# Norms and transposes of the heads moved from a stage of their own into the input projection

## What is computed

```
xn = rms_norm(x, norm_attn_g)
z  = einsum('btd,de->bte', xn, w_in)
(qa, ck, cv, sk, sv, wk, wv, ng, fq, fk, fv, ff, ga, gb) = split(z, offs, axis=-1)
qa = rms_norm(heads(qa, 8), q_norm_a_g)
sk = rms_norm(heads(sk, 2), k_norm_sel_g);  wk = rms_norm(heads(wk, 2), k_norm_win_g)
ng = sigmoid(ng)
fq = rms_norm(heads(fq, 8), q_norm_b_g);    fk = rms_norm(heads(fk, 8), k_norm_b_g)
logf = log_sigmoid(ff + b_forget)
```

## Time and profile before

| | |
|---|---|
| median of 3 runs | 964.01 us (961.81 to 964.22) |
| the profiled execution | 960.74 us, span 958.0 us |
| TensorE busy | 862.8 us, 90% of the span |
| VectorE busy | 529.6 us, 55% |
| ScalarE busy | 366.2 us, 38% |
| GpSimd busy | 158.3 us, 17% |
| mean granted TensorE clock | 0.969 |

### The profile page before, as it was taken

The page is one execution under the profiler, slowest core; times in us unless marked ns, Lnnn a source line. Parts: engine busy times, 40 slices in busy tenths (PEclk is TensorE's granted clock), DMA queues, the critical chain, the costliest instruction groups (busy, mean ns, idle before and its releaser), DMA issues. The chain is left out here.

```text
span 958.0 us, 18143 instructions
## 1 busy us (share of the span) xinstructions
PE 862.8 (90%) x7225; PEld 708.5 (74%) x7225; DVE 529.6 (55%) x982; ACT 366.2 (38%) x657; POOL 158.3 (17%) x261
## 2 busy tenths in 40 slices
PE   2899638879999999999999978899979999999996
PEld 1788427778988997665665546899569898899984
DVE  5544377863353386674456634564755665565654
ACT  2232365543242332453223441443334443444430
POOL 0000313301112112323344430000001111010100
PEclk9899878999999999999999999999979999999999
DMA  6342196116532447999999997878034644465411
GB/s 212 122 153 92 28 282 228 45 53 154 155 133 90 177 164 318 358 328 346 414 410 416 396 400 267 244 211 298 11 103 159 199 155 131 149 205 171 131 44 59
DMA packets 90590, 191.86 MB, mean 200 GB/s; under 512 B 7418, under 2 KB 68634, under 8 KB 78138
## 3 DMA queue, kind: packets, MB, share of 16 engines
q0 software_dynamic: 15408, 106.04, 28.9%
q1 hardware_dynamic: 73820, 84.43, 28.5%
q10 hardware_dynamic: 1296, 0.45, 0.2%
HBM read 187.44 MB, written 7.64 MB: 204 GB/s over the span
## 5 line engine op out<-in xcount | busy, mean ns | idle before, releaser
L1472 PEld LDWEIGHTS banks<-consts_base,stream_rows 128*128 128x128 f32 x672 | 73.2, 141 | 31.0 <-issue 28.2
L1719 ACT ACTIVATE keys_turned<-banks 128x512 f32<-128x512 f32 x94 | 54.8, 596 | 100.6 <-PE banks L1472 98.3
L258 PE MATMUL banks<-tokens_turned_high,w_gates_high 128*128 128x288 f32 x288 | 86.4, 300 | 3.5 <-PEq L191 2.3
L1472 PE MATMUL banks<-consts_base,stream_rows 128*128 128x128 f32 x672 | 82.5, 275 | 4.7 <-PEq L191 1.7
L259 PE MATMUL banks<-tokens_turned_low,w_gates_high 128*128 128x288 f32 x288 | 85.3, 296 | 0.0
L1011 PE MATMUL banks<-chunks_turned_high,cmp_w_high 64*128 64x256 f32 (+1 forms) x512 | 77.3, 296 | 5.3 <-DVE cmp_w_low L251 2.7
L260 PE MATMUL banks<-tokens_turned_high,w_gates_low 128*128 128x288 f32 x272 | 81.6, 300 | 0.0
L1011 PE MATMUL banks<-chunks_turned_low,cmp_w_high 64*128 64x256 f32 (+1 forms) x512 | 74.3, 284 | 0.0
L1011 PE MATMUL banks<-chunks_turned_high,cmp_w_low 64*128 64x256 f32 (+1 forms) x512 | 74.2, 283 | 0.0
L1700 DVE COPY keys_turned<-banks 128x512 f32<-128x512 f32 x74 | 50.3, 690 | 28.5 <-PE banks L1472 21.5
L251 DVE TENSOR_TENSOR chunks_turned_low<-banks,chunks_turned_high 128x512 fp32r<-128x512 f32 x64 | 41.1, 684 | 42.3 <-ACT chunks_turned_high L246 42.3
(11 more groups left out here) (445 smaller groups left out, 2110.6 us busy)
## 6 DMA issues: line engine op xcount, KB each, us to landing
w_up_gate<-in_w_up SPq DMA_DIRECT2D x12, 1024.0 KB, 7.3
w_up_gate<-in_w_gate SPq DMA_DIRECT2D x12, 1024.0 KB, 9.9
w_down<-in_w_down SPq DMA_DIRECT2D x12, 1024.0 KB, 5.1
w_in_slot<-in_w_in SPq DMA_DIRECT2D x8, 1424.0 KB, 6.2
w_gates<-in_w_in SPq DMA_DIRECT2D x10, 512.0 KB, 7.4
cmp_w<-in_cmp_w_k SPq DMA_DIRECT2D x4, 512.0 KB, 20.2
cmp_w<-in_cmp_w_v SPq DMA_DIRECT2D x4, 512.0 KB
stream_rows<-in_state_win_k SPq DMA_DIRECT2D x8, 256.0 KB
```

Of the source, the lines that this page charges most:

```text
L258: nc.tensor.matmul(out, lh, rh, start=start, stop=False, **kw)
L1472: ins = nc.tensor.transpose(bank(t)[:, q * P:(q + 1) * P], src, ident)
L1719: copy = lambda a, b: nc.scalar.activation(a, b, ACT.Copy)
```

## The change

`stage_heads` is gone. Chunks of the projection come in the order 3, 4, 5, 6, 0, 1, 2, 7, so that the forget-branch queries (FQ), its keys (FK), the other queries (QA) and the two other keys (KK) are complete after the third, fourth, sixth and seventh chunk. The loop of chunks is written out. Each chunk folds its own sample rows between its two prompt tiles. Squares, sums, roots, scalings and transposes of a group follow in the programs of the engines during the next chunks; KK is turned after the last chunk, and the turned forget-branch keys are evacuated by ScalarE. Row numbers are worked out after the second chunk.

In the token stage each row tile has a semaphore of its own, only the scaling waits for the gain, and ScalarE makes the high part of the first chunk as its last step. The loads of gains and the small loads of the compression network are issued during the first chunks, the masks of the prompt stage after the last chunk's load. GpSimd sets the sample rows to zero; its four gathers wait until the last chunk's queries are turned, since they write where the `w_in` slots now lie.

`load_w1` opens SyncE's program of the prompt stage. The forget gate's exponential and logarithm stand at the start of ScalarE's program there, its subtraction before the fourth unit on DVE, its running sums before the thirteenth unit on PE. The store of `logf` comes last, and GpSimd's copy of those columns waits for it, ahead of the gathers of old forget gates.

```diff
-def stage_tokens(c, w, w_loaded):
+def stage_tokens(c, z_at, w, w_loaded, wh, high):
...
-            sp.dma_start(x[:, 0:2, :], d["x_prompt"].rearrange("b (t p) d -> p (b t) d", p=P)).then_inc(tokens_in, 16)
-            sp.dma_start(x[0:NS, 2, :], d["x_sample"].rearrange("b s d -> (b s) d")).then_inc(tokens_in, 16)
-            sp.dma_start(gain[:, :], d["norm_attn_g"].to_broadcast([P, D])).then_inc(tokens_in, 16)
+            for t in range(2):
+                sp.dma_start(x[:, t, :], d["x_prompt"][0, t * P:(t + 1) * P, :]).then_inc(tokens_in[t], 16)
+            sp.dma_start(x[0:NS, 2, :], d["x_sample"].rearrange("b s d -> (b s) d")).then_inc(tokens_in[2], 16)
+            sp.dma_start(gain[:, :], d["norm_attn_g"].to_broadcast([P, D])).then_inc(gain_in, 16)
...
+                load_w_in(c, sp, w, w_loaded, u, ORDER[u] * ZC)
...
+            act.wait_ge(w_loaded[0], 16)
+            split_high(nc, wh[0][:, :, :], w[0][:, :, :]).then_inc(high, 1)
...
-            dve.wait_ge(tokens_in, 48)
...
+                dve.wait_ge(tokens_in[t], 16)
...
+            dve.wait_ge(gain_in, 16)
...
-            dve.wait_ge(pages_in, 16 * DB)
...
+ORDER = (3, 4, 5, 6, 0, 1, 2, 7)
...
+    groups = {"FQ": ((O_FQ, NH),), "FK": ((O_FK, NH),), "QA": ((O_QA, NH),), "KK": KK}
+    complete = {"FQ": 2, "FK": 3, "QA": 5, "KK": 6}
...
+                sp.wait_ge(z_sums, 3 * n - 5)
+                sp.wait_ge(low, n - 1)
+                load_w_in(c, sp, w, w_loaded, n % 2, at(n))
+                if n == 2:
+                    chunks.load_small(sp)
+            c.load_prompt(sp)
...
+            nc.gpsimd.memset(z[:, 2, :], 0.0).then_inc(zeroed, 1)
             nc.gpsimd.memset(c.qp[:, :, :], 0.0)
             nc.gpsimd.memset(c.fqp[:, :, :], 0.0)
...
+            pool.wait_ge(low, NZC)
+            pool.wait_ge(z_sums, 3 * NZC - 2)
+            pool.wait_ge(heads_turned, number["QA", 2])
             for m in range(NB):
                 chunks.gather(m)
...
+                    ins = nc.tensor.transpose(U[bank][:, r * P:(r + 1) * P], src, c.k("ident"))
+                ins.then_inc(heads_turned, 1)
...
+                u, tok = n % 2, slice(t * P, (t + 1) * P)
+                for k in range(KD):
+                    m = product(nc, U[3 * u + t][:, 0:ZC], (c.fTh[:, k, tok], c.fTl[:, k, tok]), (wh[u][:, k, :], wl[u][:, k, :]),
+                                start=(k == 0), stop=(k == KD - 1))
+                m.then_inc(z_sums, 1)
...
+            for n in range(NZC):
+                u = n % 2
+                if n >= 2:
+                    pe.wait_ge(z_out[0], 2 * n - 2)
+                    pe.wait_ge(z_out[1], n - 1)
+                    pe.wait_ge(fold_out, n - 1)
+                pe.wait_ge(w_loaded[u], n // 2 * 16 + 16)
+                for k in range(KD):
+                    g = k % 4
+                    m = nc.tensor.matmul(U[3 * u + 2][32 * g:32 * g + 32, 0:ZC], c.xsT[:, k, :], w[u][:, k, :], start=(k < 4), stop=(k >= 4))
+                m.then_inc(z_sums, 1)
+                pe.wait_ge(low, n + 1)
+                tokens(n, 0)
+                pe.wait_ge(z_out[0], 2 * n + 1)
+                nc.tensor.matmul(U[3 * u + 2][0:NS, 0:ZC], c.k("fold"), part[u], start=True, stop=True).then_inc(folded, 1)
+                if n == 5:
+                    turn(("FQ", 2))
+                if n == 6:
+                    turn(("FK", 1))
+                    turn(("FK", 2))
+                if n == 7:
+                    for t in range(3):
+                        turn(("QA", t))
+                    turn_tails()
+                tokens(n, 1)
+                if n == 1:
+                    move_row_numbers()
+                if n == 4:
+                    turn(("FQ", 0))
+                    turn(("FQ", 1))
+                if n == 5:
+                    turn(("FK", 0))
+            turn_nsa_keys()
...
+            def square(group):
...
+                act.wait_ge(fold_out, n + 1)
+                if rank[group]:
+                    act.wait_ge(sumsq, rank[group])
                 for t in range(3):
...
+                    for j, (off, heads) in enumerate(groups[group]):
+                        ins = nc.scalar.activation(sq[:, t, j * heads:(j + 1) * heads, :], by_head(t, off, heads), ACT.Square)
+                ins.then_inc(squares, 1)
+
+            def root(group):
+                act.wait_ge(sumsq, rank[group] + 1)
+                lo, n = rs_at[group], sum(heads for _, heads in groups[group])
+                nc.scalar.activation(rs[:, :, lo:lo + n], rs[:, :, lo:lo + n], ACT.Sqrt, scale=1.0 / HD, bias=c.eps[:, :]).then_inc(roots, 1)
...
+            for n in range(NZC):
+                if n == 5:
+                    queries("FQ", 0)
+                if n == 6:
+                    fox_keys(0)
+                if n + 1 < NZC:
+                    split(n + 1)
+                if n == 3:
+                    square("FQ")
+                    root("FQ")
+                if n == 4:
+                    square("FK")
+                    root("FK")
+                if n == 5:
+                    queries("FQ", 1)
+                    queries("FQ", 2)
+                if n == 6:
+                    square("QA")
+                    root("QA")
+                    fox_keys(1)
+                    fox_keys(2)
+                if n == 7:
+                    square("KK")
+                    root("KK")
+                    for t in range(3):
+                        queries("QA", t)
...
+                        nc.scalar.activation(chunks.tails[0:HD, m, :, 0:2], U[2][0:HD, m * 2 * CS:(m + 1) * 2 * CS].rearrange("p (x s) -> p s x", x=2), ACT.Copy)
+                    nc.scalar.activation(z[:, :, O_NG:O_NG + 3 * NH], z[:, :, O_NG:O_NG + 3 * NH], ACT.Sigmoid).then_inc(branch_gates, 1)
+                rows1(n)
...
+            def sample_part(n):
+                dve.wait_ge(z_sums, 3 * n + 1)
+                if n >= 2:
+                    dve.wait_ge(folded, n - 1)
+                nc.vector.tensor_copy(part[n % 2], U[3 * (n % 2) + 2][:, 0:ZC]).then_inc(z_out[0], 1)
+
+            def rows0(n):
+                dve.wait_ge(z_sums, 3 * n + 2)
+                nc.vector.tensor_copy(z[:, 0, cols_of(n)], U[3 * (n % 2)][:, 0:ZC]).then_inc(z_out[0], 1)
...
+            def sum_squares(group):
+                dve.wait_ge(squares, rank[group] + 1)
+                lo, n = rs_at[group], sum(heads for _, heads in groups[group])
+                nc.vector.tensor_reduce(rs[:, :, lo:lo + n], sq[:, :, 0:n, :], AX.X, ALU.add).then_inc(sumsq, 1)
...
+            split(0)
+            for n in range(NZC):
+                sample_part(n)
+                if n == 5:
+                    gain_keys("FK")
+                if n + 1 < NZC:
+                    split(n + 1)
+                if n == 1:
+                    row_numbers()
+                if n == 2:
+                    dve.wait_ge(rows_moved, 1)
+                    nc.vector.tensor_copy(c.quarter_row[:, :], U[7][:, 2 * P:2 * P + DB])
+                if n == 3:
+                    sum_squares("FQ")
+                if n == 4:
+                    sum_squares("FK")
+                if n == 6:
+                    sum_squares("QA")
+                if n == 7:
+                    sum_squares("KK")
+                rows0(n)
+                sample_rows(n)
+                if n == 3:
+                    scale("FQ")
+                if n == 4:
+                    scale("FK")
+                if n == 6:
+                    scale("QA")
+                if n == 7:
+                    scale("KK")
+                    gain_keys("KK")
+            forget_parts()
...
-            load_constants(sp)
+            chunks.load_w1(sp, 0)
...
-                                 ("fox_k", O_FK, FW), ("fox_v", O_FV, FW), ("logf", O_FF, NH), ("win_k", O_WK, KVW), ("win_v", O_WV, KVW)):
...
+                if name == "logf":
+                    sp.wait_ge(logf_ready, 1)
...
+                if off == O_FF:
+                    pool.wait_ge(logf_ready, 1)
...
+                if n == 12:
+                    pe.wait_ge(logf_ready, 2)
...
+                    nc.tensor.matmul(c.ps[6][:, NH:2 * NH], up[:, 0:P], lf[:, 1], start=False, stop=True).then_inc(cum_ready, 1)
...
+            nc.scalar.activation(c.forget_abs[:, :, :], c.forget_abs[:, :, :], ACT.Exp, scale=-1.0).then_inc(fl_ready, 1)
+            act.wait_ge(fl_ready, 1)
+            nc.scalar.activation(c.forget_abs[:, :, :], c.forget_abs[:, :, :], ACT.Ln, bias=1.0).then_inc(fl_ready, 1)
...
-            dve.wait_ge(masks_in, 16)
-            dve.wait_ge(cum_ready, 1)
-            link(nc.vector.tensor_copy(cq[:, :, :], c.ps[6][:, 0:2 * NH].rearrange("p (t h) -> p t h", t=2)))
+            dve.wait_ge(c.prompt_in, 16)
...
+                if n == 3:
+                    ff = z[:, :, O_FF:O_FF + NH]
+                    dve.wait_ge(fl_ready, 2)
```

(55 more changed lines are left out.)

386 lines of the change are left out of this document (167 added, 219 removed).

## The result

The changed kernel took **945.63 us** (median; 944.90 to 945.72, four runs) against 964.12 us for the kernel before (961.81 to 964.96, four runs): ratio 0.9824, 95% interval 0.9803 to 0.9845, 18.5 us less. The forecast was 939.3, 24.7 less. The profiled execution took 945.58 us, its span is 943.7, mean clock 0.976.

The account below looks back on a forecast made before the run. PE bounds the projection, while DVE and ScalarE take turns in the heads stage. Terms -23.3 up to the prompt stage's start, then -2.6 and +1.2, make -24.7: from 964.0 to 939.3 us, range for 8 in 10 933 to 946.5.

Parts of the forecast that it names:

- step 3: End of the projection: gathers end in time, prompt stage starts at 117.0 instead of 140.3 us; sum so far -23.3.
- queue rival: Projection chunks: group work waiting in DVE's and ScalarE's queues holds PE, some 8 us, giving 947; chance 0.12.
- Step 1: Token stage: DVE's first low part starts at once, first token matmul at 26.1 instead of 29.3 us; -3.2.
- Step 2: Projection chunks: folds, transposes and row numbers paid whole on PE; last token matmul ends at 113.5 us, +9.7.
- bounded this only on the side of a gain: First chunk, within the token step: up to 1.4 us more gain if PE's clock rises sooner.
- Step 4: Prompt stage: first exponential at +4.4 instead of +7.0 us, -2.6; added running sums and small operations, +1.2.
- rival by which table switches leave idle time: ScalarE's four exposed table loads: idle stretches of up to 1.4 us each, giving 944.8; chance 0.04.

Follow-up runs that it names:

- e1: The changed kernel with GpSimd's four gathers moved from the end of the projection to the prompt stage; 935.42 us, ratio 0.9727.
- e4: The kernel before with the token stage's part of the change alone, zeroing of `z` still on VectorE; 960.61 us, ratio 0.9991.
- e5: e4 with the zeroing of z's sample rows moved from VectorE to GpSimd at the projection's start; 960.52 us, ratio 0.9960.
- s14: The kernel of e1 run again, unedited, beside the changed kernel on one chip; 935.43 us, ratio 0.9719.
- e11: The kernel of e1 run again, unedited, in another set; 941.57 us, ratio 0.9763.
- e2: The changed kernel with only two of the four gathers moved to the prompt stage; 939.28 us, ratio 0.9769.
- e3: The kernel before with one added wait that holds its four gathers until near the heads stage's end; 976.58 us, ratio 1.0148.
- e8: e1 with four plain 1 MB loads added, issued by GpSimd at the projection's end; 947.65 us, ratio 0.9853.
- e9: e1 with four plain 1 MB loads added, issued by SyncE at the projection's end; 942.77 us, ratio 0.9787.
- s13: The changed kernel run again, unedited, beside the kernel of e1 on one chip; 945.31 us, ratio 0.9820.

## Why the prediction was off by 6 us

**Where it failed: step 3**, in the sentence "POOL's four gathers ... start once QA is turned and end before that", which put their cost at nothing. Their issue did end before (115.3), their landing did not. The prompt stage came at 125.25 instead of 117.0, 8.2 us late; e1 took the gathers out of this place and the stage started at 117.37. The step counted GpSimd as an engine with 4.0 us of work, where the barrier counts it until its transfers are in. The trace of the kernel before would have given it: its gathers took 9.4 us to land by the median and 14.3 at most, which from an issue at 114.35 gives 124 to 129. None of the rivals had this mechanism. The range (933 to 946.5) reached 945.6 because of the queue rival, which didn't come, so it is luck that the measured time lies inside it.

**Step 1 was right as a sum and incomplete as a reason.** First token matmul forecast at 26.1, measured 26.12; ScalarE's high part forecast at 19.0, measured 19.59. The text said that what is won is that the low part starts at once. It does so only because the zeroing of `z` has left VectorE (e4: -0.8 us without that, e5: -2.9 with it).

```profile
19.59 2.58 ACT L246 ACTIVATE w_in_high<-w_in_slot 128x2848 fp32r<-128x2848 f32 x1 [2.44 <-DMA w_in_slot<-in_w_in]
23.35 2.58 ACT L246 ACTIVATE w_in_high<-w_in_slot 128x2848 fp32r<-128x2848 f32 x1 [1.19 <-DMA w_in_slot<-in_w_in]
...
22.94 3.12 DVE L251 TENSOR_TENSOR w_in_low<-w_in_slot,w_in_high 128x2848 fp32r<-128x2848 f32 x1 [4.94 <-PEq L191]
...
26.12 0.66 PE L258 MATMUL banks<-w_in_high,tokens_turned_high 128*128 128x356 f32 x1 [0.58 <-DVE w_in_low L251]
```

**Step 2 was right from the second chunk on.** Last token matmul forecast to end at 113.5, measured 113.82 + 0.33 = 114.15. The first chunk ends at 37.09 where 38.59 - 3.2 + 0.75 = 36.14 was forecast, 0.95 late, of which the others give 0.3 back: its token matmuls follow each other every 0.295 us, the spacing of the lower clock level, from 26.12 to 30.73, for 4.6 us; in the kernel before that phase was 2.8 us long. The forecast had bounded this only on the side of a gain. The other chunks took 77.06 us where 77.35 was forecast. In them PE is busy throughout, at clock 1.00, so the group work on ScalarE and VectorE held it up nowhere, the sixth chunk included; the rival of the queues didn't come. The end of the slow phase, and the terms of the sum:

```profile
30.73 0.33 PE L258 MATMUL banks<-w_in_high,tokens_turned_high 128*128 128x356 f32 x1
...
96.13 0.79 PE L495 MATMUL banks<-h_rows,consts_base 128*32 128x356 f32 x2
96.84 1.09 PE L439 MATMUL banks<-consts_base,z 128*128 128x128 f32 x8
```

A fold costs 0.79 (0.7 and the switch to the next shape, forecast 0.75), and eight transposes 1.09, that is 0.136 each (forecast 0.125 and 0.1 for a switch).

**Step 3 apart from the gathers was right.** Table load stands ahead of ScalarE's last copy, that copy to 114.85, the gate's operations from 114.94, copies of the keys to 116.9: 117.7 with the forecast's 0.75 for the barrier. In e1, whose last token matmul ends 0.3 earlier, the stage starts at 117.37.

**Step 4 was right.** First exponential forecast 4.4 us into the stage, measured 129.61 - 125.25 = 4.36. The stage took 66.65 us against 67.80, -1.15 where the forecast said -1.4. SyncE's stores (the last one issued 38 us into the stage, 46 by the forecast) and GpSimd's gathers of the past reach nothing. The rival by which table switches leave idle time didn't come either: the loads follow the activation before within 0.02 us.

**The sum.** -24.7 forecast, +8.2 for the late start, +0.3 in step 4: -16.2, and the compression stage does start 16.2 us earlier, at 191.9 instead of 208.1. The rest of the program took 751.8 us in this profile and 749.9 in that of before; it is the same code, and between 749.2 (e1) and 753.7 (s14) in the traces of e1's kernel alone, so the 1.9 is not put down to the change. The compression stage shows where it arises: 156.64 us in the kernel before and 159.58 in the changed one, with the same instructions. For 6.8 us in the changed kernel's trace TensorE stood at the lower level, though it had been busy for all of the 14 us before that; e1's trace has no such stretch there.

```profile
191.90:351.48 159.58, 152.57 (x1894) 139.34 (x1895) 71.04 (x123) 56.73 (x95) 25.61 (x41) 0.97 0.44 141
314.00:320.80 6.80, 6.80 (x56) 6.54 (x57) 0.00 (x0) 0.00 (x0) 0.00 (x0) 0.50 0.00 0
```

```profile
183.16:339.72 156.56, 149.55 (x1894) 136.51 (x1895) 71.08 (x123) 56.70 (x95) 25.49 (x41) 0.99 0.44 144
```

In the traces of e11 and s14, the kernel of e1 again, this stage took 159.74 and 159.56 us at a clock of 0.97. The medians differ by 18.5, and the interval of the ratio reaches from 15 to 19 us; the 16.2 lie in it. Without the wait for the gathers (e1's kernel) three sets gave -26.0, -22.6 and -26.4 us for a forecast of -24.7.

**What stays open.** Why the prompt stage of kernels with the gathers in it took 65 to 67 us in some sets and 71 to 78 in others, on one chip too, with idle stretches of 1.7 to 3.7 us on VectorE for which the profile gives no true releaser; the changed kernel was seen at 66.7 and 65.8 only, and two traces don't show that it is free of them. And the price of the 2 MB weights' move to the prompt stage by itself, which is inside the -1.15, wasn't tried.

## What to carry to other kernels

Before moving an engine's last instructions to a stage's end, read what its end of stage waits for: the drain rows on the barrier's line say how long each engine's end took, also where other work covers it. Work that only issues transfers on GpSimd goes to the head of the next stage, or far enough ahead of the barrier that the last one has landed. And when a step is brought forward, look at what its engine's neighbours did in the time it used to take: a zeroing that was nearly free beside it becomes the next wait.

## What was not expected of the hardware

**GpSimd's drain at a stage's end lasts until its transfers have landed.** Issue of the last gather plus its landing, against the end of the drain: 114.35 + 9.9 = 124.25 and 124.5 (changed kernel), 112.24 + 7.7 = 119.9 and 120.0 (e2), 143.82 + 10.8 = 154.6 and 154.8 (e3), 120.09 + 14.3 = 134.4 and 134.5 (before), and for plain loads 122.7 and 122.9 (e8). The drain's recorded start is no guide: in the changed kernel it stands at 111.6, while gathers are issued up to 114.35. Whether it is the engine or its kind of queue (e8 against e9) wasn't told apart.

**SyncE's loads in flight don't hold the same barrier.** e9 shows it with 4 MB. The changed kernel shows it too: the second chunk of weights was issued in the token stage of the changed kernel, the projection opened at 22.9, and ScalarE waited for that load in the projection until 23.35 (the 1.19 us in the row above). So the load was still under way when the barrier let go.

**The same kernel can take 6 us more from one set to the next.** e1's kernel took 935.42, 941.57 and 935.43 us in three sets, each with runs within 6 us of each other and the kernel before at 961.4 to 964.2 beside it; the last two on one chip. Between the traces of e1 and e11 the prompt stage grew by 4.8 us, by the idle stretches above, and the compression by 3.2 us, at the lower clock; the rest of the program didn't grow.

**The clock row and the matmuls disagree in one window.** The first chunk's window shows clock 1.00 in the changed kernel and 0.70 in the kernel before, but in both the token matmuls start 0.295 us apart, up to 30.7 and 32.1 us, and 0.16 apart from then on. The 1.00 isn't a measurement: the first clock record in that trace stands at 30.7. In the trace of s13, the same kernel, the window reads 0.69, with the same 0.295 us between matmuls up to 31.5:

```profile
22.45:36.88 14.43, 13.81 (x65) 11.10 (x66) 7.64 (x5) 2.58 (x1) 7.72 (x8) 0.69 0.43 120
```

Where a clock row and the spacing of the matmuls disagree, a second trace of the same kernel settles it.
